# Memory turned and normed in the second expert instead of ahead of the first, and two more expert weight slots loaded aside

## What is computed

```python
# first block: 16 experts, each with three matrices of 1024 x 2816
cap = EC_CAPACITY * n_ // N_EXPERTS
g, idx = lax.top_k(jnp.swapaxes(aff, 1, 2), cap)
xs = jax.vmap(lambda ub, ib: ub[ib])(u, idx)
hid = (jax.nn.silu(jnp.einsum('becd,edf->becf', xs, w_gate))
       * jnp.einsum('becd,edf->becf', xs, w_up))
y = jnp.einsum('becf,efd->becd', hid, w_down) * g[..., None].astype(h.dtype)
# second block, in each of its two layers: keys and values of the memory
m = rmsnorm(mem, g_mem[layer])
k, v = jnp.split(m @ w_kv, 2, axis=-1)
```

## Time and profile before

| What | us |
|---|---|
| median of 3 runs (2220.53 to 2225.59) | 2224.63 |
| profiled execution, own time | 2226.71 |
| its span, first to last instruction | 2224.9 |
| PE busy in the span | 2099.5 |
| DVE, ACT, POOL busy | 780.3, 627.7, 44.6 |
| share of the chain that ended last: PE, DMA, DVE | 65%, 27%, 5% |
| data moved | 725.27 MB |

### The profile page before, as it was taken

One profiled execution on the slowest core, in us unless ns is written; L12 is line 12 of the kernel. 1 busy time (PEld: TensorE's weight loads), 2 busy tenths in 40 slices (PEclk: granted clock), 3 DMA queues, 4 the chain that ended last, 5 costly groups with the idle time before them and its releaser, 6 DMA issues.

```text
span 2224.9 us, 27202 instructions
## 1 busy us (share of the span) xinstructions
PE 2099.5 (94%) x12031; PEld 1310.1 (59%) x12031; DVE 780.3 (35%) x1144; ACT 627.7 (28%) x988; POOL 44.6 (2%) x74
## 2 busy tenths in 40 slices
PE   9999999898898999989899899889999999999999
PEld 9987443333333443434333333327889998998997
DVE  8984211011010111111011011016666565876553
ACT  6564100000000000000000000005565444965442
POOL 3201000000000000000000000000000000000000
PEclk9999999999999999999999999999999999999999
DMA  7548999999999999999999999997454656554653
GB/s 235 167 136 352 417 431 428 431 428 431 428 430 430 427 429 429 428 430 429 429 430 430 429 430 430 429 425 241 146 171 155 202 184 197 174 170 151 198 189 114
DMA packets 146527, 725.27 MB, mean 326 GB/s; under 512 B 8678, under 2 KB 106522, under 8 KB 119658
## 3 DMA queue, kind: packets, MB, share of 16 engines
q1 hardware_dynamic: 145224, 721.53, 81.1%
q0 software_dynamic: 640, 1.37, 0.2%
q10 hardware_dynamic: 546, 0.63, 0.1%
HBM read 722.44 MB, written 1.07 MB: 325 GB/s over the span
## 4 chain that ended last, share of the span: by engine, by line
PE 65%; DMA 27%; DVE 5%; ACT 1%; issue 1%; SPq 1%; DVEq 0%; ACTq 0%
PE bank L1394 24%; PE bank L1266 18%; DMA weight_ring<-in_w_gate_dram 10%; DMA weight_ring<-in_w_up_dram 9%; DMA weight_ring<-in_w_down_dram 8%; PE bank L1349 6%; PE bank L1233 5%; PE bank L1425 3%; DVE weights_ring L2480 1%; PE bank L1197 1%; PE bank L1082 1%; DVE arena L2540 1%; PE bank L1324 1%; PE bank L1611 1%; PE bank L1741 1%
## 5 line engine op out<-in xcount | busy, mean ns | idle before, releaser
L1266 PE MATMUL bank<-weight_ring,arena 128*64 128x506 f32 x3024 | 634.6, 565 | 65.4 <-DMA weight_ring<-in_w_up_dram 42.6
L1266 PEld LDWEIGHTS bank<-weight_ring,arena 128*64 128x64 f32 x3024 | 219.8, 135 | 464.6 <-issue 374.6
L1349 PE MATMUL bank<-weight_ring,arena 128*64 128x512 f32 x1408 | 323.2, 610 | 40.1 <-DMA weight_ring<-in_w_down_dram 40.0
L2915 DVE TENSOR_TENSOR weights_ring<-weight_ring,weights_ring 128x2048 fp32r<-128x2048 f32 x110 | 249.7, 2289 | 126.3 <-ACT weights_ring L2174 125.9
L1394 PE MATMUL bank<-input_high,weights_ring 128*128 128x256 f32 x1920 | 248.3, 281 | 0.9 <-issue 0.9
L1349 PEld LDWEIGHTS bank<-weight_ring,arena 128*64 128x64 f32 x1408 | 99.2, 140 | 244.3 <-issue 185.5
L1394 PEld LDWEIGHTS bank<-input_high,weights_ring 128*128 128x128 f32 x1920 | 234.6, 188 | 2.9 <-issue 2.6
L2174 ACT ACTIVATE weights_ring<-weight_ring 128x2048 fp32r<-128x2048 f32 x109 | 205.8, 1908 | 60.2 <-DMA weight_ring<-in_w_ffn_down_dram 41.1
L2872 DVE TENSOR_TENSOR arena<-arena,bank 128x512 f32<-128x512 f32 x48 | 33.0, 688 | 498.9 <-PE bank L1233 498.9
L2070 ACT ACTIVATE arena<-bank 128x506 f32<-128x506 f32 (+1 forms) x48 | 23.5, 563 | 398.3 <-PE bank L1266 398.3
L1394 PE MATMUL bank<-input_low,weights_ring 128*128 128x256 f32 x960 | 132.3, 279 | 0.0
(11 more groups left out here) (431 smaller groups left out, 2080.0 us busy)
## 6 DMA issues: line engine op xcount, KB each, us to landing
weight_ring<-in_w_down_dram SPq DMA_DIRECT2D x62, 2816.0 KB, 21.8
weight_ring<-in_w_up_dram SPq DMA_DIRECT2D x61, 2816.0 KB, 19.5
weight_ring<-in_w_gate_dram SPq DMA_DIRECT2D x60, 2816.0 KB, 18.9
weight_ring<-in_w_ffn_gu_dram SPq DMA_DIRECT2D x44, 1024.0 KB, 5.1
weight_ring<-in_w_ffn_down_dram SPq DMA_DIRECT2D x22, 1024.0 KB, 4.9
weight_ring<-in_w_in_dram SPq DMA_DIRECT2D x16, 1024.0 KB, 5.9
arena<-in_w_xkv_dram SPq DMA_DIRECT2D x8, 2048.0 KB, 21.2
weight_ring<-in_ab_w_in_dram SPq DMA_DIRECT2D x12, 1024.0 KB, 7.7
```

The source lines that it names most:

```text
L1266: last = pe.matmul(bank[first_bank + c][MPAD * half:MPAD * half + MPAD, 0:(hi - lo) * HF], xs3[:, s, :], w[:, lo:hi, HF * half:HF * half + ...
L1349: last = pe.matmul(bank[6][MPAD * half:MPAD * half + MPAD, :], hidT[:, at:at + MPAD], W[:, j * D + 512 * half:j * D + 512 * half + 512], s ...
L2915: dve.tensor_tensor(low_slot(k), raw_slot(k), high_slot(k), ALU.subtract).then_inc(S("weights_low"), 1)
```

## The change

The memory is no longer turned ahead of the first expert. Its four groups of transposes (`memory_features`) stand behind slots 0, 2, 4 and 6 of the second expert's gate, all in bank 7. The copies and squares on ACT (`memory_taken`), the sum on PE and the norm on DVE move to the second expert as well. So the first key and value stage, (1, "gate"), leaves `KV_STAGES`, and (11, "down") comes in; the loads are still issued by the same rule. `AHEAD_SLOT` becomes 3: a fifth up slot of the first expert is loaded aside, right behind the memory. Its place in the ring is filled with a down slot earlier, and down slot 2 is loaded alone. When the first expert's up product is done, the last up slot of the second expert is loaded into the place that `ahead[0]` had (`late_up`), ahead of `kv_load(0)`, and the second expert's ring load of up pair 3 is only one slot. The rest of the diff counts semaphores.

```diff
--- before.py
+++ after.py
@@ -71,8 +71,8 @@
-KV_STAGES = [(1, "gate"), (2, "gate"), (3, "gate"), (4, "gate"), (5, "gate"), (5, "down"), (6, "down"), (7, "gate"),
-             (8, "gate"), (8, "down"), (9, "down"), (10, "gate"), (11, "gate"), (12, "gate"), (13, "gate"), (14, "gate")]
+KV_STAGES = [(2, "gate"), (3, "gate"), (4, "gate"), (5, "gate"), (5, "down"), (6, "down"), (7, "gate"),
+             (8, "gate"), (8, "down"), (9, "down"), (10, "gate"), (11, "gate"), (11, "down"), (12, "gate"), (13, "gate"), (14, "gate")]
...
@@ -279,11 +279,12 @@
         PAIRS = ESLOTS // 2
-        AHEAD_SLOT = ESLOTS // 2
-        ahead = [z(DFF, at) for at in (0, 2816, 7680, 13280)]
-        mem_squares = z(KT * 256, 10496)
-        memtok = z(2 * D, 10496)
-        mT = z(KT * 256, 5632)
+        AHEAD_SLOT = ESLOTS - 5
+        ahead = [z(DFF, at) for at in (0, 2816, 10496, 7680, 13312)]
+        late_up = z(DFF, 0)
+        memtok = z(2 * D, 5632)
+        mT = z(KT * 256, 2816)
+        mem_squares = z(KT * 256, 12288)
         before = z(P, 23344)
...
@@ -371,7 +372,7 @@
-            eng.wait_ge(landed(g), 16 * (A_USES[g] + 3 * e + use - (g >= PAIRS - 2)))
+            eng.wait_ge(landed(g), 16 * (A_USES[g] + 3 * e + use - (g == PAIRS - 2)))
...
@@ -615,7 +616,10 @@
                     sp.wait_ge(S("gate_used"), 8 * e + 2 * g + 2)
-                    pair_load("w_up", e, g)
+                    if e == 1 and g == PAIRS - 1:
+                        sp.dma_start(expert_slot(2 * g), rows_of("w_up", e)[:, 2 * g * DFF:(2 * g + 1) * DFF]).then_inc(landed(g), 16)
+                    else:
+                        pair_load("w_up", e, g)
                 next_kv_load(e, "gate")
...
@@ -634,13 +638,14 @@
             sp.wait_ge(S("r_scores"), H)
-            ahead_load(AHEAD_SLOT + 2)
+            ahead_load(AHEAD_SLOT + 3)
             sp.wait_ge(S("ret_ready"), H)
             sp.dma_start(before, t["before"]).then_inc(S("tokens_landed"), 16)
-            ahead_load(AHEAD_SLOT + 3)
+            ahead_load(AHEAD_SLOT + 4)
             sp.wait_ge(S("y_ready"), 2 * H)
             sp.dma_start(tiles(memtok, 2), mem).then_inc(S("tokens_landed"), 16)
             ahead_load(AHEAD_SLOT + 1)
+            ahead_load(AHEAD_SLOT + 2)
             for s in range(1, ESLOTS):
...
@@ -651,15 +656,19 @@
                   .then_inc(S("half_landed") if s else landed(0), 16)
+            sp.wait_ge(S("gate_used"), 3)
+            sp.dma_start(expert_slot(2), rows_of("w_up", 0)[:, 2 * DFF:3 * DFF]).then_inc(landed(1), 16)
             sp.wait_ge(S("gate_used"), 4)
-            pair_load("w_up", 0, 1)
+            sp.dma_start(expert_slot(3), rows_of("w_down", 0)[:, 3 * DFF:4 * DFF]).then_inc(landed(3), 16)
             for g in range(PAIRS - 2, PAIRS):
                 sp.wait_ge(S("gate_used"), 2 * g + 2)
                 pair_load("w_down", 0, g)
-            for g in range(PAIRS - 2):
-                sp.wait_ge(S("up_used"), 2 * g + 2)
-                pair_load("w_down", 0, g)
+            sp.wait_ge(S("up_used"), 2)
+            pair_load("w_down", 0, 0)
+            sp.wait_ge(S("up_used"), 3)
+            sp.dma_start(expert_slot(2), rows_of("w_down", 0)[:, 2 * DFF:3 * DFF]).then_inc(landed(1), 16)
             sp.wait_ge(S("up_used"), ESLOTS)
+            sp.dma_start(late_up, rows_of("w_up", 1)[:, (ESLOTS - 1) * DFF:ESLOTS * DFF]).then_inc(S("apart_landed"), 16)
             kv_load(0)
...
@@ -1151,20 +1160,23 @@
-            pe.wait_ge(S("tokens_landed"), MEM_TOKENS)
             m3 = memtok.rearrange("p (j f t) -> p j t f", j=2, t=KT)
-            for b in range(4):
-                pe.wait_ge(S("utok_taken"), b + 1)
+
+            def memory_features(b):
+
+                if b == 0:
+                    pe.wait_ge(S("tokens_landed"), MEM_TOKENS)
+                else:
+                    pe.wait_ge(S("utok_taken"), 10 + b)
                 for i in range(2):
                     for j in range(2):
-                        last = pe.transpose(bank[b][:, 256 * i + P * j:256 * i + P * j + P],
-                                            m3[:, j, 2 * b + i, :], ident[:])
+                        last = pe.transpose(bank[7][:, 256 * i + P * j:256 * i + P * j + P], m3[:, j, 2 * b + i, :], ident[:])
                 last.then_inc(S("utok_ready"), 1)
             ht3 = tiles(hT[:], KT)
             for n in range(4):
                 t, half = n // 2, n % 2
-                pe.wait_ge(S("utok_taken"), 6 + n)
+                pe.wait_ge(S("utok_taken"), n + 1)
                 for i in range(4):
...
@@ -1246,6 +1258,8 @@
                             pe.wait_ge(S("kv_taken"), kv_blocks_through(e, "gate"))
+                            if e == 1:
+                                pe.wait_ge(S("utok_taken"), 14)
                         scatter(e, s // 4)
...
@@ -1256,6 +1270,9 @@
                         w = ahead[s - AHEAD_SLOT]
+                    elif e == 1 and use == 2 and s == ESLOTS - 1:
+                        pe.wait_ge(S("apart_landed"), 16 * (ESLOTS - AHEAD_SLOT + 1))
+                        w = late_up
                     elif e == 0 and s == 1:
...
@@ -1269,6 +1286,8 @@
                         choice_rows()
+                    if e == 1 and use == 1 and s % 2 == 0:
+                        memory_features(s // 2)
                     if use == 1 and s % 2 == 0 and kv_blocks(e, "gate"):
...
@@ -1300,19 +1319,21 @@
                 last.then_inc(S("xs_ready"), 1)
-            pe.wait_ge(S("utok_taken"), 14)
+            pe.wait_ge(S("utok_taken"), 10)
             hid3 = th.rearrange("p (f j) -> p f j", j=HF)
             for e in range(EXP):
                 pe.wait_ge(S("xs_taken"), e + 2 if e else 1)
                 hidden(e, 0, "gate_used", 1)
                 if e == 0:
-                    pe.wait_ge(S("pool_steps"), 6)
+                    pe.wait_ge(S("pool_steps"), 2)
                     row_slots(0)
-                    pe.matmul(bank[7][:, 0:256], ones[:], mem_squares[:, 0:256], start=True, stop=True).then_inc(S("norm_sum"), 1)
                     pe.wait_ge(S("choice_steps"), 4)
                 hidden(e, 3, "up_used", 2)
                 pe.wait_ge(S("scatter_taken"), 4 * e)
+                if e == 1:
+                    pe.wait_ge(S("pool_steps"), 6)
+                    pe.matmul(bank[7][:, 0:256], ones[:], mem_squares[:, 0:256], start=True, stop=True).then_inc(S("norm_sum"), 1)
                 if e + 1 < EXP:
...
@@ -1327,7 +1348,7 @@
                     pe.wait_ge(S("rows_taken"), e + 3)
-                    if e == 0:
+                    if e == 1:
                         pe.wait_ge(S("norm_rstd"), 1)
...
@@ -1336,6 +1357,8 @@
                         pair_landed(pe, e, pairs, 3)
+                        if e == 0 and pairs == 1:
+                            pair_landed(pe, 0, PAIRS - 1, 3)
                         pairs += 1
...
@@ -2028,10 +2051,7 @@
                                scale=rate_cols[0:ROWS[j], j:j + 1]).then_inc(S("utok_taken"), 1)
-            for b in range(4):
-                act.wait_ge(S("utok_ready"), 6 + b + 1)
-                act.activation(mT[:, 512 * b:512 * b + 512], bank[b][:], ACT.Copy).then_inc(S("utok_taken"), 1)
-            act.wait_ge(S("utok_ready"), 14)
+            act.wait_ge(S("utok_ready"), 10)
             for n in range(4):
...
@@ -2053,10 +2073,14 @@
-            act.wait_ge(S("utok_taken"), 10)
-            m_T, m_sq = tiles(mT, KT), tiles(mem_squares, KT)
-            for q in range(4):
-                act.activation(m_sq[:, 2 * q:2 * q + 2, :], m_T[:, 2 * q:2 * q + 2, :], ACT.Square).then_inc(S("norm_squares"), 1)
+            def memory_taken():
+                for b in range(4):
+                    act.wait_ge(S("utok_ready"), 10 + b + 1)
+                    act.activation(mT[:, 512 * b:512 * b + 512], bank[7][:], ACT.Copy).then_inc(S("utok_taken"), 1)
+                act.wait_ge(S("utok_taken"), 14)
+                m_T, m_sq = tiles(mT, KT), tiles(mem_squares, KT)
+                for q in range(4):
+                    act.activation(m_sq[:, 2 * q:2 * q + 2, :], m_T[:, 2 * q:2 * q + 2, :], ACT.Square).then_inc(S("norm_squares"), 1)
...
@@ -2064,6 +2088,8 @@
             for e in range(EXP):
+                if e == 1:
+                    memory_taken()
                 exp_tanh_set()
...
```

More of the change, by code:

```diff
@@ L362, in build @@
         A_USES = [len([k for k in range(NA) if k % CSLOTS == s]) for s in range(SLOTS)]
-        B_USES = [(3 * EXP - (s >= PAIRS - 2) if s < PAIRS else 1) if s < ESLOTS else 0 for s in range(SLOTS)]
+        B_USES = [(3 * EXP - (s == PAIRS - 2) if s < PAIRS else 1) if s < ESLOTS else 0 for s in range(SLOTS)]
         LAST_ROWS = (FT - 1) * D
@@ L507, in build @@
         UTOK_BANKS = [0, 1, 2, 3, 6, 4]
-        STREAM_BANKS = [4, 0, 1, 2]
+        STREAM_BANKS = [0, 1, 2, 3]
         key_sum = rows[0]
@@ L1345, in _ @@
                         if j == FT - 1:
```

(4 more changed lines are left out.)

## The result

The changed kernel takes 2242.69 us (median of 6 runs, 2238.02 to 2244.08), the kernel before 2224.28 (6 runs, 2220.53 to 2225.59): a ratio of 1.0082, with a 95% interval of 1.0069 to 1.0095. It is 18.4 us slower. The time is 3.3 us above the 2239.4 that was forecast, and the change is 3.6 above the forecast 14.8. The profiled execution was the shortest of its runs: 2238.02 us, with a span of 2236.2.

What follows compares the result with a forecast made beforehand. From about 258 us the weight stream was taken to bound the experts, before that PE. From the median 2224.63, 5.4 us saved at the start and 20.2 lost in two stops gave +14.8, 2239.4 us, range 2231 to 2249.

Steps and rivals of the forecast that it cites:

- The start: First expert up to expert 1's gate: earlier gather, dropped sum of squares and slot brought ahead save 5.4 us (4.0 to 5.8).
- memory and stages: First expert: without the memory's transposes and sum of squares, PE releases everything 2.05 us earlier.
- the slots: Before 208 us: one ring slot is loaded early, taking 3.35 us out of the later weight stream.
- The step on the gather: Start of first expert: gather waits only for DVE's choice of rows and starts at 200.2, 1.4 us earlier.
- The second expert at no cost: Second expert: the memory work moved in costs nothing, covered by the weight stream and the up product.
- the stops behind slot 0 of experts 7 and 10: Gates of experts 7 and 10: PE waits some 17 us for a `w_xkv` load, and the stream runs dry.
- The length of a stop: Experts 7 and 10: stream time lost each time, 10.1 us (7.4 to 13.1), 20.2 us for two.
- 0.13 slower than the 6.70 of the stream, three times: 0.4: Behind each standstill PE releases three gate pairs every 6.83 us, slower than the stream, losing 0.4 us.
- It doesn't run dry again: After each standstill: PE needs 10.64 us to the next gate pair, against 20.1 us queued in the stream.
- the fast one: Experts 7 and 10: load lands with early gate pairs, stream never dry, 2219.2 us; 8 in 100.
- The dearest rival: Experts 8 and 11: stream runs dry a second time, some 6.4 us each, giving 2252 us; 6 in 100.
- the margin of 1.1 us: First gate pair of the expert after a standstill: 1.1 us said to remain before the stream runs dry again.

## Why the prediction was right

It gave 2239.4 with a range of 2231 to 2249; 2242.7 came.

- The start, -5.4: right in sum and in its parts. Measured as times of whole kernels, memory and stages gave 2.1 (forecast 2.05), the slots 3.3 (3.35), together 5.5. That they agree to a tenth is more than these measurements can tell, above all for the 2.1. The step on the gather held: it waits 0.42 us for DVE, right behind the remaining transposes. The first gate product started at 203.02 and the first gate pair of expert 1 was issued at 252.96, where 204.5 and 254.5 were given; with the 1.5 us of the mixer both are met.
- The second expert at no cost: no wait of PE for ACT, POOL or the norm is among its waits from 260 us on, but for the one of 1.9 us for DVE that was there before.
- The counting of the two stage lists, and the stops behind slot 0 of experts 7 and 10: right in place and kind. They last 19.3 and 18.5 us where some 17 stood. The sum took both ends of the first wait from the kernel before, but PE ended slot 0 of expert 7 at 761.4 instead of 775.5, 14.1 us earlier, and the load landed at 780.7 instead of 792.2, 11.5 earlier. Of the 11.5, 4.9 are a `w_xkv` load less ahead of it (three instead of four by the two lists), which the prediction didn't count; the start's 5.4 and the mixer's 1.5 are about the rest. What makes PE gain 2.6 us more than the load wasn't traced. It costs nothing, since it only lengthens a wait in which the stream moves.
- The length of a stop was the term that was mis-sized: 10.1 us forecast, 11.9 and 11.3 measured by landings, 11.8 alone in the kernel before. Its parts: from the load's landing to the first up pair's issue 7.25 forecast, 6.8 and 6.1 measured; start-up of the first pair 2.45 forecast, 2.3 and 2.5 measured. The DMA share was zero for some 7.3 us (780.7 to 788.0) and not 9: the pair's first bytes moved 0.5 us behind its issue, and the rest of the 2.3 is a slow start, 360 GB/s from 788 to 792. Of these parts only the last one fails, "0.13 slower than the 6.70 of the stream, three times: 0.4". The second and third pair behind the standstill lost 2.1 + 0.7 and 1.4 + 1.3 us, 2.8 and 2.7 instead of 0.4. The second was issued 2.2 us before the first landed, and landed 8.8 behind it. The pair of 256.52, which I had used as the upper bound for an empty queue, was in truth such a second one: the load of 245.88 ahead of it took 12.4 us and landed at 258.3, 1.8 us behind the pair's issue, and the pair came 8.6 behind that, 1.9 above its 6.7. By landings the two stops are 23.2 us where 20.2 stood, 3.0 more. By the times of whole kernels they are 23.9, 3.7 more, and that is the miss of the change (3.6). The 0.7 between the two wasn't traced; it is about the late down pairs, and below the scatter of the runs.
- "It doesn't run dry again": right, the next landing that is over 1 us late comes behind expert 10's stop.
- Of the rivals, the fast one (the load finishing with the early gate pairs) is excluded by both waits: the load landed 4.9 us behind the last gate pair at both, in the order of issue. So the trace bears out no disorder of the kind that the Trainium skill, page "DMA: Bandwidth & Descriptors", section "Queues, rings and completion order", allows for. The dearest rival, a second standstill in expert 8, didn't come; the margin of 1.1 us that the prediction set against it has no rows and no working.

## What to carry to other kernels

Where one queue is filled in the order of use, ask of every transfer: what is issued behind it, and does that wait for the engine that will stop for this one? If so, the wait costs not its own length but the time in which the queue is empty (here from the wait's end to the next issue), plus a slow start of the pairs that come next. A schedule that is moved by one place has to be counted through against the loads that follow it by another rule (here: every second stage), because one entry can put the first use of a load right behind its issue.

## What the runs showed of the hardware that was not expected

A queue that has run dry is slow for more than its first transfer. The first 2.88 MB pair landed 9.0 us after its issue, 2.3 above its bytes. The next two were issued 6.83 us apart, nearly at the stream's pace of 6.7, and were still late by 2.1 and 0.7 us. The stretches from one landing to the next (columns as above) are those of the second, third and fourth up pair:

```profile
796.50:805.30 8.80, 8.80 (x42) 4.56 (x40) 0.69 (x1) 0.00 (x0) 0.00 (x0) 1.00 0.97 386
805.30:812.70 7.40, 7.40 (x37) 2.54 (x38) 3.72 (x6) 2.75 (x4) 0.00 (x0) 1.00 0.97 390
812.70:819.30 6.60, 6.60 (x36) 2.71 (x34) 0.00 (x0) 0.00 (x0) 0.00 (x0) 1.00 1.01 434
```

In the first two the engines of the transfers count as busy for 0.97 of the time, but move 386 and 390 GB/s. So most of this loss isn't a gap between pairs but a lower rate. What in the transfer path does this was not tried.

The second block has two paces of TensorE. In the kernel before, 173 matmul records of the feed-forward part take 20.00 us, and in the changed kernel 19.30, at the same granted clock (stretch tables of the kernel before and of the changed kernel):

```profile
1740.00:1760.00 20.00, 20.00 (x173) 20.00 (x172) 10.45 (x8) 9.68 (x8) 0.00 (x0) 1.00 0.54 171
```

```profile
1754.30:1773.60 19.30, 19.30 (x173) 19.30 (x172) 10.30 (x9) 9.69 (x8) 0.00 (x0) 1.00 0.56 187
```

The code is the same in both and the faster pace lasts for some 100 us, worth some 4.3 us. The kernel with the blocks behind odd slots had it too, and the other profiled kernels did not: from the last `scatter` to the end of the span these two took 709.0 and 709.4 us, and the seven others 713.0 to 713.9. It isn't the change's doing, and it is about the size of the scatter of the runs (2238.0 to 2244.1); that it explains that scatter was not tried. It does mean that two single executions of this kernel can't be compared to better than 4 us, and the median of a few runs can be off by as much. A time taken where the experts end is free of it.
